# A trunk layer with expert retrieval: where the side work of the first 80 expert slots is placed

## The reference, cut to what matters

```
q  = (hf @ w_q).reshape(T, 8, 2, 128)                      # 8 heads
sc = einsum('thpc,pkc->thpk', q, sub_keys)                 # 2 x 128 key scores a head
v1, i1 = top_k(sc, 16)                                     # routing: top 16 of each half,
top, pos = top_k(v1[.., 0, :, None] + v1[.., 1, None, :], 16)   # then of their sums
experts, gates = cidx[pos], softmax(top)
a = gelu(einsum('cd,ced->ce', x, u[experts]))              # 16 experts a token and head
y = einsum('ce,ced->cd', gates * a, v[experts])
```

## Time and profile before

| | us |
|---|---|
| median of 3 runs | 987.9 |
| lowest and highest | 987.59, 987.97 |
| the profiled execution: its time | 986.92 |
| the profiled execution: span from first to last instruction | 984.8 |
| PE / DVE / ACT / POOL busy in the span | 819.7 / 619.5 / 408.9 / 356.1 |
| first gather issued | 319.45 |

### The profile page before, as it was taken

The page is one execution under the profiler, slowest core; times in us unless marked ns, Lnnn a source line. Parts: engine busy times, 40 slices in busy tenths (PEclk is TensorE's granted clock), DMA queues, the critical chain, the costliest instruction groups (busy, mean ns, idle before and its releaser), DMA issues.

```text
span 984.8 us, 11539 instructions
## 1 busy us (share of the span) xinstructions
PE 819.7 (83%) x3604; PEld 513.8 (52%) x3604; DVE 619.5 (63%) x1446; ACT 408.9 (42%) x1001; POOL 356.1 (36%) x301
## 2 busy tenths in 40 slices
PE   5999979999998878999889777777777777777776
PEld 5999768899976645545535222222222222222222
DVE  4434673465656884886776666666766666666454
ACT  6434453445453453454344243342442423323243
POOL 0000191013000653475565435444444444444410
PEclk9999779999999799999999999999999999999999
DMA  7887222365343998999999999999999999999995
GB/s 267 258 212 215 86 86 87 128 224 221 155 150 129 371 420 328 374 407 422 420 421 421 423 421 422 423 422 420 422 424 421 421 422 424 421 421 420 423 422 223
DMA packets 48802, 324.87 MB, mean 330 GB/s; under 512 B 5508, under 2 KB 8824, under 8 KB 10104
## 3 DMA queue, kind: packets, MB, share of 16 engines
q0 software_dynamic: 36864, 268.45, 66.0%
q1 hardware_dynamic: 11752, 55.61, 16.7%
q10 hardware_dynamic: 144, 0.26, 0.1%
HBM read 322.77 MB, written 1.54 MB: 329 GB/s over the span
## 4 chain that ended last, share of the span: by engine, by line
PE 42%; DMA 41%; DVE 6%; issue 5%; ACT 5%; POOL 1%; DVEq 0%; SPq 0%; POOLq 0%; ACTq 0%
DMA late_ring<-in_experts,expert 38%; PE y L816 12%; PE ps L583 8%; PE ps L584 8%; PE ps L585 8%; DMA arena<-in_experts,expert 2%; DVE row_max L1293 1%; ACT diag L1090 1%; DVE w_lo L1226 1%; PE ps L683 1%; POOL late_ring L1693 1%; PE ps L671 1%; ACT acts L1083 1%; DVE arena L1289 1%; DMA raw<-in_panels 1%
## 5 line engine op out<-in xcount | busy, mean ns | idle before, releaser
L816 PE MATMUL y<-late_ring,diag 128*128 128x512 f32 x500 | 238.2, 616 | 72.8 <-ACT diag L1090 72.8
L816 PE MATMUL y<-arena,diag 128*128 128x512 f32 x508 | 236.3, 604 | 56.5 <-ACT diag L1090 55.5
L1693 POOL DMA_INDIRECT arena<-in_experts,expert x128 | 154.0, 1203 | 238.9 <-PE y L816 121.2
L1693 POOL DMA_INDIRECT late_ring<-in_experts,expert x128 | 156.6, 1223 | 164.1 <-PE y L816 132.3
L1571 DVE CUSTOM_DVE_ANT_0 arena<-arena 128x1024 f32<-128x1024 f32 x128 | 156.8, 1225 | 88.1 <-DMA arena<-in_experts,expert 88.0
L1571 DVE CUSTOM_DVE_ANT_0 late_ring<-late_ring,arena 128x1024 f32<-128x1024 f32 x128 | 156.3, 1223 | 88.5 <-DMA late_ring<-in_experts,expert 85.8
L816 PEld LDWEIGHTS y<-late_ring,diag 128*128 128x128 f32 x500 | 92.3, 193 | 209.7 <-ACT diag L1090 113.1
L816 PEld LDWEIGHTS y<-arena,diag 128*128 128x128 f32 x508 | 92.6, 191 | 191.0 <-issue 97.9
L1075 ACT ACTIVATE acts<-dots 128x2 f32<-128x2 f32 x126 | 25.6, 203 | 339.8 <-DVE dots L1571 339.7
L1226 DVE TENSOR_TENSOR w_lo<-raw,w_hi 128x2048 fp32r<-128x2048 f32 x41 | 96.1, 2347 | 96.5 <-ACT w_hi L895 96.5
L583 PE MATMUL ps<-h_hi,w_hi 128*128 128x256 f32 x400 | 118.7, 297 | 1.3 <-DVE h_lo L1258 1.3
(11 more groups left out here) (238 smaller groups left out, 993.0 us busy)
## 6 DMA issues: line engine op xcount, KB each, us to landing
raw<-in_panels SPq DMA_DIRECT2D x42, 1024.0 KB, 4.9
arena<-in_panels SPq DMA_DIRECT2D x4, 1024.0 KB, 6.9
arena<-line_scratch SPq DMA_DIRECT2D x8, 320.0 KB, 9.1
arena<-in_experts,expert POOLq DMA_INDIRECT x128, 31.7
late_ring<-in_experts,expert POOLq DMA_INDIRECT x128, 31.7
x<-in_x SPq DMA_DIRECT2D x2, 512.0 KB, 3.7
arena<-in_mem SPq DMA_DIRECT2D x1, 1024.0 KB, 7.1
out<-x SPq DMA_DIRECT2D x3, 256.0 KB, 7.1
```

The source lines that it names most:

```text
L816: mm = pe.matmul(y[:, t, half * 512:(half + 1) * 512], diag[:, s % DIAGS, :], row[:, at:at + 512], start=False, stop=False, skip_group_che ...
L1693: nc.gpsimd.indirect_dma_start(out=slot(u, s), out_offset=None, in_=experts, in_offset=bass.IndirectOffsetOnAxis(ap=expert[:, parity, s:s ...
```

## The change

The side work of the first five units is no longer placed unit by unit but over the 80 slots (DVE) and 40 groups (PE, ACT) by tables.

* Routing (DVE): unit 1 over slots 0 to 10, unit 2 over 11 to 21, unit 3 over 26 to 37, unit 4 over 38 to 50, unit 5 over 51 to 65, unit 6 over 66 to 79.
* Gates (DVE) after slots 13, 25, 42, 56, 70, and after slot 5 in place of 3 in the loop of the later units.
* DVE's part of panels 3 to 7 after slots 15, 27, 39, 52, 66; ACT's part after groups 4, 11, 17, 23, 30.
* PE's product with panels 3 to 7 after groups 8, 14, 20, 27, 34 (group 8 is the first of unit 1), its key scores two groups later; ACT takes the query two and the scores three groups after the product.
* The second tile of head 2: product before group 4 in place of 3, turn after 5 in place of 4, scores after 6 in place of 5; ACT takes them after 4, 5 and 7, and scales the second tile's rows after 7.
* Softmaxes (ACT) after groups 3, 8, 17, 23, 31, 38.
* Buffers 6 and 7 join at slots 52 and 68 in place of 48 and 64.

No instruction is added or removed, apart from their order.

```diff
--- before.py
+++ after.py
@@ -61,14 +61,24 @@
 AHEAD = 2
 SOFTMAX_AFTER = 6
 QUERIES_FIRST = 3
-SPLIT_AT_SLOT = 5
-SPLIT_AFTER_GELU = 1
-FIRST_ROUTE = [range(2 * s, 2 * s + 2) if s < 8 else range(0) for s in range(TOPK)]
-GATES_AT_SLOT = 3
-UNIT_1_ROUTE = [range(0) if s < 6 else range(2 * (s - 6), 2 * (s - 5)) if s < 12 else range(s, s + 1) for s in range(TOPK)]
-NEXT_ROUTE = [range(3 * (s - 10), min(3 * (s - 9), 16)) if s >= 10 else range(0) for s in range(TOPK)]
-QUERY_AFTER_GROUP = 3
-SCORES_AFTER_GROUP = 5
+GATES_AT_SLOT = 5
+
+
+def over_slots(unit, first, last):
+
+    n = last - first + 1
+    return {first + i: [(unit, k) for k in range(16 * i // n, 16 * (i + 1) // n)] for i in range(n)}
+
+
+ROUTE_AT = {}
+for part_of_route in (over_slots(1, 0, 10), over_slots(2, 11, 21), over_slots(3, 26, 37), over_slots(4, 38, 50),
+                      over_slots(5, 51, 65), over_slots(6, 66, 79)):
+    ROUTE_AT.update(part_of_route)
+GATES_AT = {13: 1, 25: 2, 42: 3, 56: 4, 70: 5}
+SPLIT_LO_AT = {15: 3, 27: 4, 39: 5, 52: 6, 66: 7}
+SPLIT_HI_BEHIND = {4: 3, 11: 4, 17: 5, 23: 6, 30: 7}
+QUERY_BEHIND = {8: 3, 14: 4, 20: 5, 27: 6, 34: 7}
+SOFTMAX_BEHIND = {3: 2, 8: 3, 17: 4, 23: 5, 31: 6, 38: 7}
 LAST_SPLIT = PANELS.index("qpeer2")
 OWN_PLACE = SPLIT_RING
 QUERY_UNITS = PEER_HEADS - QUERIES_FIRST
@@ -81,7 +91,7 @@
 EARLY_BEHIND = {"kv0": "qpeer5", "kv1": "qpeer6", "kv2": "qpeer2", "qpeer1": "qpeer7"}
 RAW_LOADED = [name for name in PANELS if name not in LOADED_EARLY]
 FIRST_BUFFERS = [0, 8, 2, 3, 4, 5, 9, 10, 11, 12, 13]
-JOINS = {48: 6, 64: 7, ALL_FROM + 5: 1, ALL_FROM + 6: 14, ALL_FROM + 7: 15}
+JOINS = {52: 6, 68: 7, ALL_FROM + 5: 1, ALL_FROM + 6: 14, ALL_FROM + 7: 15}
 
 
 def ring_order():
@@ -837,28 +847,20 @@
             for step in (query_product, query_turn, query_scores):
                 for h in range(2):
                     step(h, 1)
-            for g in range(TOPK // GROUP):
-                if g == 0:
+            for i in range(QUERY_UNITS * TOPK // GROUP):
+                if i == 0:
                     query_product(2, 0)
-                if g == 3:
+                if i == 4:
                     query_product(2, 1)
-                use_group(0, 0, g)
-                if g in (0, 4):
-                    query_turn(2, g // 4)
-                if g in (1, 5):
-                    query_scores(2, g // 5)
-                if g == 6:
-                    channels_by_tokens(f"qpeer{QUERIES_FIRST}", h_pair)
-            for u in range(1, QUERY_UNITS):
-                later = QUERIES_FIRST + u
-                for g in range(TOPK // GROUP):
-                    use_group(u, 0, g)
-                    if u == 1 and g == 0:
-                        key_score(QUERIES_FIRST)
-                    if g == QUERY_AFTER_GROUP:
-                        channels_by_tokens(f"qpeer{later}", h_pair)
-                    if g == SCORES_AFTER_GROUP:
-                        key_score(later)
+                use_group(i // (TOPK // GROUP), 0, i % (TOPK // GROUP))
+                if i in (0, 5):
+                    query_turn(2, i // 5)
+                if i in (1, 6):
+                    query_scores(2, i // 6)
+                if i in QUERY_BEHIND:
+                    channels_by_tokens(f"qpeer{QUERY_BEHIND[i]}", h_pair)
+                if i - 2 in QUERY_BEHIND:
+                    key_score(QUERY_BEHIND[i - 2])
             with pe.Fori(QUERY_UNITS, PEER_HEADS) as u:
                 for g in range(TOPK // GROUP):
                     use_group(u, 0, g)
@@ -1135,37 +1137,28 @@
             for take_step in (take_query_tile, take_turned_query, take_scores_tile):
                 for h in range(2):
                     take_step(h, 1)
-            for g in range(TOPK // GROUP):
-                weigh(0, g)
-                if g == 0:
+            for i in range(QUERY_UNITS * TOPK // GROUP):
+                weigh(i // (TOPK // GROUP), i % (TOPK // GROUP))
+                if i in SOFTMAX_BEHIND:
+                    expert_softmax(SOFTMAX_BEHIND[i])
+                if i == 0:
                     take_query_tile(2, 0)
                     take_turned_query(2, 0)
-                if g == 1:
+                if i == 1:
                     take_scores_tile(2, 0)
-                if g == 2:
-                    expert_softmax(2)
-                if g == 4:
+                if i == 4:
                     take_query_tile(2, 1)
-                    split_panel(PANELS.index(f"qpeer{QUERIES_FIRST}"))
+                if i in SPLIT_HI_BEHIND:
+                    split_panel(PANELS.index(f"qpeer{SPLIT_HI_BEHIND[i]}"))
+                if i == 5:
                     take_turned_query(2, 1)
-                if g == 5:
+                if i == 7:
                     take_scores_tile(2, 1)
                     scale_rows(1)
-            expert_softmax(3)
-            for u in range(1, QUERY_UNITS):
-                later = QUERIES_FIRST + u
-                for g in range(TOPK // GROUP):
-                    weigh(u, g)
-                    if u == 1 and g == 0:
-                        take_query(QUERIES_FIRST)
-                        take_scores(QUERIES_FIRST)
-                    if g == SPLIT_AFTER_GELU:
-                        split_panel(PANELS.index(f"qpeer{later}"))
-                    if g == SCORES_AFTER_GROUP:
-                        take_query(later)
-                    if g == SOFTMAX_AFTER:
-                        expert_softmax(u + AHEAD + 1)
-                take_scores(later)
+                if i - 2 in QUERY_BEHIND:
+                    take_query(QUERY_BEHIND[i - 2])
+                if i - 3 in QUERY_BEHIND:
+                    take_scores(QUERY_BEHIND[i - 3])
             with act.Fori(QUERY_UNITS, UNITS - AHEAD) as u:
                 for g in range(TOPK // GROUP):
                     weigh(u, g)
@@ -1582,18 +1575,13 @@
                 nc.vector.tensor_scalar(diag[:, s % DIAGS, :], ident[:], acts[:, s:s + 1], gate_now[:, s:s + 1],
                                         ALU.mult, ALU.mult).then_inc(last_diag, 1)
 
-            def use_unit(u, t, late_query=None, routed=True):
+            def use_unit(u, t, routed=True):
 
                 for s in range(TOPK):
                     dot(u, t, s)
                     if s == GATES_AT_SLOT:
                         gate_weights(u + 1)
-                    if s == SPLIT_AT_SLOT and late_query is not None:
-                        split_panel(PANELS.index(f"qpeer{late_query}"))
-                    if routed and isinstance(u, int) and u == 1:
-                        for k in UNIT_1_ROUTE[s]:
-                            route_step_of(u + AHEAD, k)
-                    elif routed:
+                    if routed:
                         route_step_of(u + AHEAD, s)
 
             route_first()
@@ -1604,18 +1592,14 @@
             rows_rstd(1)
             gate_weights(0)
             dve.wait_ge(h_rows_ready, 1)
-            for s in range(TOPK):
-                dot(0, 0, s)
-                for k in FIRST_ROUTE[s]:
-                    route_step_of(1, k)
-                if s == 9:
-                    gate_weights(1)
-                for k in NEXT_ROUTE[s]:
-                    route_step_of(2, k)
-                if s == 12:
-                    split_panel(PANELS.index(f"qpeer{QUERIES_FIRST}"))
-            for u in range(1, QUERY_UNITS):
-                use_unit(u, 0, QUERIES_FIRST + u)
+            for n in range(QUERY_UNITS * TOPK):
+                dot(n // TOPK, 0, n % TOPK)
+                if n in GATES_AT:
+                    gate_weights(GATES_AT[n])
+                if n in SPLIT_LO_AT:
+                    split_panel(PANELS.index(f"qpeer{SPLIT_LO_AT[n]}"))
+                for u, k in ROUTE_AT.get(n, ()):
+                    route_step_of(u, k)
             dve.wait_ge(taken["act"], taken_count(f"key_score{PEER_HEADS - 1}"))
             with dve.Fori(QUERY_UNITS, PEER_HEADS) as u:
                 use_unit(u, 0)
```

## The result

The changed kernel takes 979.1 us in the median of 4 runs (977.24 to 981.7); the kernel before, timed beside it, 987.75 us in the median of 4 (986.83 to 987.97). The ratio is 0.9916, 95% interval 0.9892 to 0.994. The forecast was 979.4, 0.3 us off. The profiled execution took 981.7 us with a span of 979.6; it is the slowest of its four, for a reason that lies ahead of the change: its first gather went out at 322.16, not at 319.45, and PE began its first panel product at 15.35 in place of 13.70, so that it was 1.7 us behind from there on. From the first gather to the end it took 979.6 - 322.16 = 657.4 us, the kernel before 984.8 - 319.45 = 665.4.

The account below looks back on a forecast made before the run. The queue of gathers was taken to bound the kernel: 9.1 us lost in two poor windows, less 0.6 for PE's clock and a narrow lead, gives 8.5, so 987.9 becomes 979.4 us; range 978.0 to 984.0.

Parts of the forecast that it names:

- What bounds: The DMA queue of gathers sets the program's end; two poor windows, 380 to 440 us, lose 9.1 us together.
- The term for PE's clock and the narrow lead: At gather 29 the lead of 8.2 us might shrink to 6.5 if PE's clock falls; 0 to 1.5 lost, 0.6 taken.
- The walk: PE and ACT followed group by group: group 8 ends at 383.2, panel 3's product at 389.4, gather 29 issued at 391.9.
- The sum: 9.1 us recovered less 0.6 gives 8.5, so 987.9 falls to 979.4 us.
- hole: Gather rate falls to 302 GB/s from 380 to 405 us, where the queue runs short; 7.1 us lost.
- one chain: Panel 3's product between groups 6 and 7 delays ACT by 7.17 us, then DVE by 15.71, emptying the ring of 11.
- rival A: The hole only shrinks, as panel 3's product still blocks the ring; half of 9.1 us remains, 983.4 us; chance 0.17.
- The second dip: The lower rate after 400 us, 398 GB/s from 405 to 440, is the hole's echo from late, bunched buffers; 2.0 us.
- The threshold: A gather's lead is its work queued ahead; above about 8 us nothing is lost, below it the rate sinks.
- B: Rival: the loss returns as dips at panels 4 and 5, following after 12 slots, not 16; 987 to 988 us; chance 0.06.
- C: Rival: PE does not work off its backlog; panels 3, 4 and 5 each open a 3.7 us hole; 989.9; chance 0.09.
- Descriptors: Port sharing with DVE may lengthen some gather issues near 391 by 1 to 2 us; the 0.6 us sum stays.

Follow-up runs that it names:

- a2: The changed kernel run again unchanged, to see its spread; median 979.18 us, ratio 0.9914 to the kernel before.
- f1: The changed kernel with the second tile of head 2 back in its old, earlier places; 983.11 us, ratio 0.996 to the kernel before.
- e1: The changed kernel with PE's product with panel 3 back behind group 6, in unit 0; 979.06 us, ratio 0.9924 to the kernel before.
- e2: The changed kernel with panel 4's low part on DVE after slot 22 and ACT's high part behind group 10, so DVE stops again; 979.18 us.
- e3: The changed kernel with head 3's scores made right behind its product and taken by ACT before it weighs group 9; 985.76 us.
- e7: The kernel before with only head 3's scores later: made behind group 9, taken by ACT behind group 10; 984.09 us.
- f2: The kernel before with only the second tile of head 2 in its new, later places; 984.4 us, ratio 0.9972.
- f3: The kernel before with both the later scores of head 3 and the second tile of head 2 in its new places; 983.75 us.
- e4: The changed kernel with panel 3's product made twice in a row behind group 8, the first result overwritten; 983.26 us.
- e6: The changed kernel with 9 buffers in place of 11 for the first 52 slots; 982.49 us, ratio 0.9938 to the kernel before.
- e8: The changed kernel with buffers 6 and 7 joining at slots 48 and 64 again; 979.37 us, ratio 0.9936 to the kernel before.

## Why the prediction was right

*What bounds.* Right: the queue of gathers sets the end, and the 9.1 us that the windows gave are what came back in the rate: 9.2 us lost from 340 to 440 before, 0.2 after. In time it was less: 656.3 - 648.4 = 7.9 us by the stretch in the first pair of profiles, 8.5 with a2's 647.8; 8.65 by the medians beside the result, 8.0 in the second set. Why a little less comes back in time than in the rate is not shown.

*The term for PE's clock and the narrow lead, 0.6 us.* Too large: 0. The clock did not fall: PE stood 1.80 us and not 2.93 in front of group 6, and f1, which has the 2.93 us back, has the lower clock back too. And gather 29's time to landing was 9.2 us or more and not 8.2. The walk itself held. Shifted by the 2.7 us of the later start, group 8 was to end at 385.9 and the product 6.15 later, near 392.1; the groups behind it started at 391.24. POOL issued gather 29 at 393.89 (walk: 394.6). ACT waited for the scores (1.78 us) and DVE for them at slot 26 (3.15 us, walk: 4), hidden by PE's backlog as argued.

*The sum.* That it met the median within 0.3 us is in part luck. The 0.6 us were taken off for a loss that did not come; without them the same sum says 978.8. They happen to stand where the time gives back 0.5 to 1 us less than the rate.

*The cause.* Here the prediction had the right hole and a wrong weight on its parts. It named one chain: product between groups 6 and 7, ACT's wait for the scores, DVE's stop. Undone one at a time in the changed kernel: the product's place 0 (e1; 1.4 us of queue), a DVE stop of 6.36 us 0 (e2), the coupling of scores and weigh 6.6 us (e3), and the second tile of head 2, which the walk moved along without giving it a price, 3.9 us (f1). These don't add, as only the latest gather counts. In the kernel before, the scores alone bring 3.1 us (e7), the second tile alone 2.7 (f2), both together 3.3 (f3), by the medians. The prediction called the DVE stop the larger part, in rival A; nothing measured supports that.

*The second dip.* The prediction called it an echo of the hole. It is for the most part not: e7 keeps the hole and loses nearly all of the dip, and f2 and f3, which differ in the scores alone, have 295 and 378 GB/s in the two windows of 5 us from 400 in the one and 415 and 419 in the other. It was gather 29's own wait behind group 9, which PE began after a wait of 2.26 us for the diagonals that ACT weighs behind the scores.

*The threshold.* "Above about 8 us nothing is lost" holds roughly. The table says it better: in nine kernels, from 2.4 to 10.2 us of lateness, the loss by the rate is the lateness less 0 to 1.0 us, and at or below zero it is nothing. In part that is bookkeeping, as both numbers are from the same trace. The medians are not, and they follow in the main: over 979.18 they lie 8.0 us (before), 6.6 (e3), 5.2 (f2), 4.9 (e7), 4.6 (f3), 4.1 (e4), 3.9 (f1), 3.3 (e6) and nothing (e1).

*Rivals.* A and B did not come: no window after 340 is below 415 GB/s. C's mechanism, a backlog not worked off from product to product, fits what f3 shows at a spacing of five groups and does not come at six: after panel 4's product in the changed kernel no gather is late. *Descriptors:* right, nothing in the time.

## What to carry to other kernels

When a queue of transfers bounds a ring of buffers, compute for each transfer how late it is issued against the unbroken pace. In these kernels the loss was about the largest of these, so fixing a smaller one shows nothing, and fixing the largest gains only down to the next. Look there for waits in which one engine's side work stands ahead of its part in the main chain and depends on an engine with a backlog: take results one or two steps later than they can be ready. Side work itself cost nothing here where its spacing let the backlog be worked off.

## What was not expected of the hardware

TensorE's idle times of 2.93 us (before and f1) and 3.68 us (e3) were each followed by a stretch at the lower clock, and those of 1.80 and 1.90 us in front of groups 6 and 2 of the changed kernel were not. Between them it went either way: 2.26 us in front of group 9 before were followed by it, and of two waits at one and the same place of the later units the kernel before has 0.54 behind 2.33 us (over the 3.5 us from 583.90), the changed kernel 1.00 behind 2.32 us (from 578.54). The slower records cost 1.3 us in f1 and 3.0 in e3, of which 1.9 reached gather 29. And executions differ by up to 4 us in when the first gather goes out (318.80 in e8, 322.79 in e7), though the code ahead of it is the same. That is more than most of what was to be told apart here; counting from the first gather takes it out.
